# Gates with tokens on the partitions in two blocks, values ahead of keys, embedding pieces in pairs of one bank

## What is computed

```python
for i in range(2):
    h = rms_norm(x, g_pre_mix[i])
    if i == 0: mix = short_conv_mixer(h, ...)
    else:
        k, v = split(rms_norm(x, g_kv) @ w_kv)           # 1024 key and 1024 value columns
        mix = diff_attention(h, k, v, dist_bias, w_q, lambda, ...)   # 8 heads, keys of 2 x 64
    x = x + rms_norm(mix, g_post_mix[i])
    x = x + rms_norm(conv_ffn(rms_norm(x, g_pre_ffn[i]), ...), g_post_ffn[i])
    gate = sigmoid(rms_norm(x, g_pre_ple[i]) @ w_gate)   # 1024 x 1024
    x = x + rms_norm(gate * (p_i @ w_proj), g_post_ple[i])   # p_i: 256 features, w_proj 256 x 1024
```

## Time and profile before

| | us |
|---|---|
| median of 3 runs | 1263.34 (1263.01 to 1263.54) |
| the profiled execution, span | 1261.9 |
| TensorE busy | 1231.6 |
| VectorE busy | 908.1 |
| ScalarE busy | 737.1 |

### The profile page before, as it was taken

The page is one execution under the profiler, slowest core; times in us unless marked ns, Lnnn a source line. Parts: engine busy times, 40 slices in busy tenths (PEclk is TensorE's granted clock), DMA queues, the critical chain, the costliest instruction groups (busy, mean ns, idle before and its releaser), DMA issues.

```text
span 1261.9 us, 24318 instructions
## 1 busy us (share of the span) xinstructions
PE 1231.6 (98%) x10110; PEld 1206.4 (96%) x10110; DVE 908.1 (72%) x1571; ACT 737.1 (58%) x1257; POOL 6.4 (1%) x16
## 2 busy tenths in 40 slices
PE   8999999999999999999999999999999999999997
PEld 8889799999999999999999999999888899999997
DVE  6896566665446776444876899966788768999656
ACT  6753456664445765334555666655766866665655
POOL 1000000000000000000000000000000000000000
PEclk9999999999999999999999999999899999999999
DMA  7223244555552655553663666574364236665640
GB/s 275 72 101 105 64 164 148 192 181 180 174 168 98 216 186 185 184 184 126 218 195 119 193 194 199 159 238 134 120 225 159 89 117 192 193 189 188 215 141 34
DMA packets 59753, 205.51 MB, mean 163 GB/s; under 512 B 6739, under 2 KB 9340, under 8 KB 59516
## 3 DMA queue, kind: packets, MB, share of 16 engines
q1 hardware_dynamic: 57536, 201.21, 49.0%
q10 hardware_dynamic: 2108, 2.75, 0.7%
HBM read 202.87 MB, written 1.06 MB: 162 GB/s over the span
## 4 chain that ended last, share of the span: by engine, by line
PE 85%; DVE 8%; ACT 4%; issue 1%; DMA 1%; DVEq 0%; ACTq 0%
PE PS L368 69%; PE PS L413 6%; DVE WL L353 2%; PE PS L380 2%; DMA RAW<-wpack 1%; ACT WH L346 1%; PE PS L462 1%; PE PS L2450 1%; ACT EE L2608 1%; PE PS L520 1%; PE PS L2517 0%; PE PS L688 0%; DVE X L1905 0%; ACT L532 0%; PE PS L402 0%
## 5 line engine op out<-in xcount | busy, mean ns | idle before, releaser
L353 DVE TENSOR_TENSOR WL<-RAW,WH 128x1024 fp32r<-128x1024 f32 (+2 forms) x387 | 460.6, 1195 | 211.3 <-ACT WH L346 210.8
L346 ACT ACTIVATE WH<-RAW 128x1024 fp32r<-128x1024 f32 (+2 forms) x387 | 392.3, 1033 | 218.6 <-PE PS L368 184.8
L368 PE MATMUL PS<-UH,WH 128*128 128x256 f32 (+1 forms) x1464 | 415.7, 284 | 7.6 <-DVE WL L353 3.8
L368 PE MATMUL PS<-UL,WH 128*128 128x256 f32 (+1 forms) x1464 | 414.9, 283 | 0.0
L368 PE MATMUL PS<-UH,WL 128*128 128x256 f32 (+1 forms) x1464 | 414.7, 283 | 0.0
L368 PEld LDWEIGHTS PS<-UH,WH 128*128 128x128 f32 x1464 | 276.6, 189 | 8.6 <-issue 3.4
L368 PEld LDWEIGHTS PS<-UH,WL 128*128 128x128 f32 x1464 | 276.9, 189 | 0.0
L368 PEld LDWEIGHTS PS<-UL,WH 128*128 128x128 f32 x1464 | 275.2, 188 | 0.0
L368 PE MATMUL PS<-HL,WH 128*128 128x272 f32 (+1 forms) x512 | 145.8, 285 | 0.0
L368 PE MATMUL PS<-HH,WH 128*128 128x272 f32 (+1 forms) x512 | 145.6, 284 | 0.0
L368 PE MATMUL PS<-HH,WL 128*128 128x272 f32 (+1 forms) x512 | 145.4, 284 | 0.0
(11 more groups left out here) (409 smaller groups left out, 2066.1 us busy)
## 6 DMA issues: line engine op xcount, KB each, us to landing
RAW<-wpack SPq DMA_DIRECT2D x361, 512.0 KB, 4.2
RAW<-wpack SPq DMA_DIRECT2D x18, 384.0 KB, 3.5
RAW<-wpack SPq DMA_DIRECT2D x6, 256.0 KB, 2.7
C<-cst SPq DMA_DIRECT2D x1, 1072.0 KB, 5.9
HB<-bias_rows ACTq DMA_DIRECT2D x1, 1024.0 KB, 5.3
out<-X SPq DMA_DIRECT2D x4, 256.0 KB, 2.3
X<-xin ACTq DMA_DIRECT2D x2, 272.0 KB, 6.0
X<-xin SPq DMA_DIRECT2D x2, 272.0 KB, 5.9
```

The lines of the kernel that those rows point to most:

```text
L346: a.e.activation(WH[n % NH][:, 0:w], RAW[n % NR][:, 0:w], ACT.Copy).then_inc(*a.mark("wh", n))
L353: v.e.tensor_tensor(WL[n % NH][:, 0:w], RAW[n % NR][:, 0:w], WH[n % NH][:, 0:w].bitcast(f32), ALU.subtract).then_inc(*v.mark("wl", n))
L368: ins = t.e.matmul(o, part(n, hw, kw, a, b), x(kx), start=first and not i and not p, stop=last and i == len(kcs) - 1 and p == 2)
```

## The change

**Embedding.** Two pieces share a bank, with tokens on the partitions: for each block i of 128 tokens 256 columns of w_proj move. Six pieces are now done ahead of the FFN and two ahead of the gate, and ScalarE copies a pair in one instruction. The turn of the banks is set again at a later unit of the FFN.

**Gate.** A unit is now two 128-row pieces of w_gate by 512 columns. The tokens of a block are stationary and 512 weight columns move. First both blocks for the columns 0 to 511 (h = 0), then block 0 and then block 1 for the columns 512 to 1023 (h = 1). The norm's factor is a scale of the sigmoid, per partition, so that the spread and the multiplication L2349 go; the sum of squares over the features is an accumulator of one ScalarE and one VectorE instruction per block. Each block is then scaled and turned by eight transposes (`gate_turned`) into features on partitions and added to X (`gate_added`). In layer 0, block 0 is turned inside the last products of block 1; block 1 is turned inside the first value products.

**Values ahead of keys.** Behind the gate of layer 0 come four value units (heads 0 to 3, block 0 and then block 1), then four key units; the keys of heads 4 to 7 take the place of the first four half value units in the loop over the heads, in bank 1 or 2.

```diff
+            pairs_of_rows("v", "w_kv_2", None, 1024, 1536)
+            proj("k", "w_kv_2", None, 0, 512)
+            for h in range(8):
+                proj("q", "w_q_2", 0, 128 * h, 128 * h + 128)
+                if h < 4:
+                    proj("k", "w_kv_2", None, 512 + 128 * h, 640 + 128 * h)
...
 # tensor_ffn
-            embed(2, 5)
+            embed(2, 6)
...
-                        if (u, m) == (3, 0):
+                        if (u, m) == (4, 0):
                             banks.go_on((banks.at["root", prev] + 1) % 8)
...
-            keep_going(t, 2, f"f{layer}")
+            keep_going(t, 8, f"f{layer}")
...
+            for k in range(8):
+                gate_rows(0, k, (0, 1))
+            for k in range(8):
+                if k == 2:
+                    root_sum(t, st, 0, S, ("rs", st))
+                gate_rows(1, k, (0,))
+            if layer:
+                for k in range(8):
+                    gate_rows(1, k, (1,), 0, 256)
+            for k in range(8):
+                if k == 6 - 2 * layer:
+                    gate_turned(t, layer, 0)
+                gate_rows(1, k, (1,), 256 * layer, 512)
 # scalar_ffn
-            act_split(a, n0 + NH)
+            act_split(a, n0 + NH + 4)
             root_sqrt(a, st, S)
             preload(a, ACT.Sigmoid)
...
+            gate_sigmoid(a, layer, 0, 0, 0, 512)
+            gate_sigmoid(a, layer, 1, 0, 0, 512)
             gate_square(0)
             gate_square(1)
+            gate_sigmoid(a, layer, 0, 1, 0, 512)
+            preload(a, ACT.Sqrt, 61)
+            gate_root(a, layer, 0)
+            gate_scale_first(a, layer, 0)
+            preload(a, ACT.Sigmoid, 62)
 # vector_ffn
+            dve_split(v, n0 + NH + 4)
             root_recip(v, st, S)
-            dve_split(v, n0 + NH)
+            gate_product(v, layer, 0, 0, 0, 512)
+            gate_product(v, layer, 1, 0, 0, 512)
+            gate_first_sum(v, layer, 0)
+            gate_first_sum(v, layer, 1)
+            gate_product(v, layer, 0, 1, 0, 512)
+            gate_squares(v, layer, 0)
+            gate_recip(v, layer, 0)
+            gate_scale_second(v, layer, 0)
 # tensor_diff, after the two blocks of values (gate_turned(t, 0, 1) ahead of k = 6 of block 0)
+            pair, spare = banks.at["nt", 0, 1], banks.at["nt", 0, 0]
+            for j in range(4):
+                b = banks.put(t, (spare, spare + 1, *rest)[j], ("k", j), ("kh", j))
...
+                if j == 1:
+                    banks.go_on(pair)
+                    root_sum(t, "kv", 0, S, ("rk", "kv"))
             b = banks.take(t, ("lam",), ("lame",))
 # scalar_diff (high(i, j) waits for X of block i, piece j, and makes UH; 128 columns)
+            act_split(a, n0)
+            for j in range(3):
+                high(0, j)
+            gate_sigmoid(a, 0, 1, 1, 0, 512)
+            preload(a, ACT.Sqrt, 63)
+            high(0, 3)
+            gate_root(a, 0, 1)
+            high(0, 4)
+            gate_scale_first(a, 0, 1)
...
             for j in range(8):
                 split_hi(a, ("qx", j), XH[:, j, :], X_(j), g("gpm1", j))
+                if j == 1:
+                    root_sqrt(a, "kv", S)
+                if j in (2, 4, 6):
+                    act_split(a, n0 + 2 + j // 2)
             a.e.dma_start(HB[:, :, :], rows).then_inc(*a.mark_dma("hb"))
             root_keep(a, "kv", 0, S)
+            for i in range(2):
+                a.e.activation(V[:, i, 0:512], PS[:, banks.at["v", 0, i], :], ACT.Copy, scale=rooted("kv", 1 + i))
+            act_split(a, n0 + 4 + NH)
             scalar_embed(a, 1)
             a.wait_ge("dif", "lam")
             a.e.activation(SM[:, 38:40], PS[:, banks.at["lam",], 0:2], ACT.Exp)
 # vector_diff
+            for j in range(4):
                 key(j)
+                dve_split(v, n0 + NH + 1 + j)
             vector_embed(v, 1)
 # tensor_end, scalar_end, vector_end
+            keep_going(t, 20)
+            for j in range(8):
+                ins = t.e.matmul(..., MR[:, 1, 128 * j:128 * j + 128], DG, start=True, stop=True)
```

More of the change, by code:

```diff
@@ L2089, in embed @@
                 for j in range(j0, j1):
[L2090 to L2096, removed]
+                    i, x, at = j % 2, (0, 0, 1, 2)[j // 2], (0, 256, 0, 0)[j // 2]
+                    n = unit_at["ple", 3 * layer + x]
+                    b = banks.at["ple", layer, j - 1] if i else banks.take(t, ("ple", layer, j), ("pe", layer, j + 1))
+                    t.wait_ge("wl", n)
+                    t.wait_ge("ul", "p", layer)
+                    for k in range(2):
+                        for p, (y, hw) in enumerate(((PH, 1), (PL, 1), (PH, 0))):
+                            ins = t.e.matmul(PS[:, b, 256 * i:256 * i + 256], y[:, k, 128 * i:128 * i + 128], part(n, hw, k, at, at + 256),
+                                             start=k == 0 and p == 0, stop=k == 1 and p == 2)
+                    if i:
+                        ins.then_inc(*t.mark("ple", layer, j))
+                    if j in (3, 5, 7):
                         sig.also(("used", n), ("ple", layer, j))
@@ L2141, in tensor_ffn @@
             root_end(t, f"f{layer}", 1, S)
-            embed(5, 6)
+            embed(6, 7)
             root_spread(t, f"f{layer}", S)
-            embed(6, 8)
-            keep_going(t, 2, f"f{layer}")
+            embed(7, 8)
+            keep_going(t, 8, f"f{layer}")
             n0 = unit_at["gate", 8 * layer]
[L2147 to L2163, removed]
-                            *t.mark("gate", layer, u, m))
-                for m in range(2):
-                    sig.also(("used", n + m), ("gate", layer, u, m))
@@ L2440, in value @@
             def value(s):
+                if s < 4:
+                    key(4 + s, banks.put(t, BV + s % 2, ("k", 4 + s), ("kh", 4 + s)))
+                    return
                 uu, half = s // 2, s % 2
@@ L2566, in scalar_diff @@
             a.e.dma_start(HB[:, :, :], rows).then_inc(*a.mark_dma("hb"))
-            root_sqrt(a, "kv", S)
-            act_split(a, n0 + NH + 1)
             root_keep(a, "kv", 0, S)
-            act_split(a, n0 + NH + 4)
+            a.wait_ge("rr", "kv")
+            for i in range(2):
+                a.wait_ge("dif", "v", 0, i)
+                a.e.activation(V[:, i, 0:512], PS[:, banks.at["v", 0, i], :], ACT.Copy, scale=rooted("kv", 1 + i)).then_inc(
+                    *a.mark("v", 0, i))
+            act_split(a, n0 + 4 + NH)
             scalar_embed(a, 1)
```

353 lines of the change are left out of this document (202 added, 151 removed).

## The result

| | us |
|---|---|
| before, median of 5 runs on the same chip | 1263.34 (1262.01 to 1263.54) |
| after, median of 5 runs | 1267.79 (1267.06 to 1269.39) |
| ratio | 1.0042, interval 1.0029 to 1.0054 |
| span of the profiled execution after | 1265.3 |

The changed kernel is 4.45 us slower. The forecast was 1272, in a range from 1263 to 1276; the sign was right, the size twice too large.

What follows compares the result with a forecast made beforehand. It took TensorE's matmuls (1416 in 167.29 us) to bound the kernel; +0.8 + 11.8 - 1.5 + 1.5 - 3.6 = +9.0 on the 1263.3 median gave 1272.3, say 1272 us, in a range from 1263 to 1276.

Steps and rivals of the forecast that it cites:

- Step 1: Embedding: six pieces instead of five ahead of each FFN, +0.4 us a layer, +0.8 in all (bounds 0 and 1.4).
- Step 2: Gate of layer 0: two late-loaded units hold the root until 893.5; TensorE stands still 6.2 us inside the gate.
- Step 3: Values behind layer 0's gate: start 906.4, waits of 1.9 and 1.0 us between block 0's pieces, end 921.4.
- Step 4: Keys behind the values: K2's high part stands behind the root, a wait of 1.7 us; keys and `lam` end 936.6.
- Step 5: First query: waits for `lam`'s exponential behind six splits, starts at 946.7 (bounds 944.5 and 948) against 934.92, +11.8 us.
- The clock term: Behind the hole ahead of query 0: about 4 us of work at half pace, +1.5 us (0 to 2).
- The covered waits: Behind query 0: the idle 0.47 us at 941.20 and 1.01 at 951.90 go, -1.5 us.
- Step 6: Last gate and tail: no wait for block 0, last addition 1255.5 against 1259.1, -3.6 us (bounds -2.5 and -4.5).
- the forecast proper: Whole kernel: the forecast's own band of 1266.5 to 1276 us, given a chance of 0.64.
- the signs that it had named: TensorE idle about 6 us ahead of the transposes and 10 ahead of query 0; root behind two copies waiting for DMA.
- The table loads: New ScalarE table switches: the skill's draining would add some 4 us, making 1276; left out, 1.28 us a load taken.

Runs made afterwards that it cites:

- Experiment 2: Changed kernel with the gate root behind four unit splits instead of six, units 9 and 10 split later: 1266.47 us, ratio 1.0028.
- experiment 4: Kernel before with the new form in layer 1 alone (embedding pairs, gate by blocks, new tail), layer 0 old: 1259.04 us, ratio 0.9966.
- experiments 1 to 3: Changed kernel with `lam` in bank 5 (1260.97 us), with the gate root ahead of two later unit splits (1266.47), and with both edits (1258.69).
- experiment 1: Changed kernel with the product `lam` put in bank 5 instead of bank 0: 1260.97 us, ratio 0.9987.
- experiments 2, 6, 7 and 8: The sixth: on version 3, K2's split ahead of the `kv` root (1257.40 us), then VectorE's keys before splits (1256.14), then query 1 and head 0 earlier (1258.08).
- version 3: Changed kernel with both edits, `lam` in bank 5 and the gate root ahead of the splits of units 9 and 10: 1258.69 us, ratio 0.9968.
- the best version: version 3 with K2's split ahead of the `kv` root and VectorE's key and query 0 copies ahead of later low parts: 1256.14 us, ratio 0.9951.
- experiment 7: the best version with the third and fourth value unit splits moved between the pieces of the additions: 1260.03 us, ratio 0.9982.
- experiment 8: Kernel before with `lam` in bank 0: 1268.52 us; the same with the bank turn kept: 1262.74; changed kernel with `lam`'s exponential ahead of five splits: 1261.48.

## Why the prediction was right or wrong

The forecast's times count from a gate of layer 0 that starts at 873.69. In the trace after it starts at 872.52, so 1.2 us of each difference between two such times is not the forecast's.

**Step 1, embedding: too high.** +0.8 forecast. The FFN of layer 0 starts 0.5 us later measured from the short convolution's output, that of layer 1 0.25 later, and each gate then starts 0.3 earlier: about +0.2. The fillers that took the place of two pieces ahead of the gate gave a little back; I had put them at 0.

**Step 2, gate of layer 0: right in kind, a little high.** Two copies wait for DMA ahead of the root, as written. The second copy ended and the root began at 891.79 where I had 893.5; from the gate's start this is 19.3 us against 19.8. The wait ahead of the transposes is 5.26 (forecast 6.2). Unit 9 was loaded from 885.25 and copied from 888.43, 3.2 us, where I had taken 4.5. But unit 10 decided when the root came: it was issued at 886.39 and copied from 890.83, 4.4 us later, the lower end of what I had allowed it. Experiment 2, which brought the transposes 3.1 us forward, shows what that was worth: 1.8 us of time (1.1 of distance), not 3.5 to 5, since the rest went into what stood behind it.

**Step 3, values: right.** Start 904.48 (906.4), waits of 1.40 and 0.49 (1.9 and 1.0), end 919.1 (921.4). My VectorE addition of 128 columns from PSUM, taken as 0.27, has that pace in the tail: eight in 2.16 us.

**Step 4, K2: right.** A wait of 1.43 against 1.7, for the reason given.

**Step 5, first query: the right place and reason, 30% too large.** The bank count by hand was right: `lam` in the query's bank. The wait is 8.36 us (10), query 0 at 942.71 (946.7); from the gate's start the loss is 8.96 us (11.8). Of the missing 2.8 us half came before the load: N+10 was issued at 935.01, which is 62.5 us behind the gate's start where I had 63.9, since the root, the values and K2 were each a little earlier. The other 1.2 are the load: it was copied at 939.60, 4.6 us after its issue, where I had taken 5.8 from a load that had stood behind others. The clock term (+1.5) measured 2.0: 20 products from 942.71 to 947.14 took 0.213 us each where 0.117 is the pace. The covered waits (-1.5) were right, and the two terms of opposite sign made the stretch behind the query even, to within half a microsecond.

**Step 6, tail: right, a little low.** -3.6 forecast, -4.5 in the traces, -4.3 by experiment 4. The products ended as before; the chain behind them took 6.6 us where I had 6.9, and the span ended 2.4 us behind the last addition instead of 2.8 as before.

**Sum.** +0.2 + 9.0 + 0 - 4.5 = +4.7 against a measured +4.45; forecast +9.0. The missing 4.3 are 2.8 at query 0, 0.9 in the tail and 0.6 at the embedding. The three errors have the same sign, so nothing cancelled; the term that was sized worst is that of query 0. The bounds of step 5 (944.5 to 948) were too narrow: both ends assumed a late load, and from the gate's start query 0 came 0.6 us below the lower one. The result lies 1.3 us above the lower end of the forecast proper (1266.5), and the range given (1263 to 1276) held because it was wide. What speaks for the working are the signs that it had named, the two waits with their releasers and the two copies ahead of the root, and not the time.

**The table loads.** In the changed kernel a table load runs from 892.05 to 893.33 and the next instruction starts at 893.35. The Trainium skill, "ScalarE: Activation LUTs", section "What ACT_TABLE_LOAD costs", adds some 1.38 us of draining to each switch. The trace again does not agree, and the 1276 that this would have given did not come.

**What I had not asked.** Whether the loss could be had back. I treated the late exponential and the late root as what the change is; experiments 1 to 3 show that they are two places in an order, worth 9.3 us, and that the form itself is neutral in layer 0 (within 0.3 us in the traces) and worth 4.3 us in the tail.

## What to carry to other kernels

Where an engine runs in written order, a wait needs two things: a late event and something that is queued or banked behind it. Look for what else shares the bank or the queue of a small side product, and move that, before the big work is moved. A rotating allocator couples far places: an edit that takes one slot less moved a 4.9 us wait into a stage 80 us later, so compare the whole timeline, not the edited stretch. And a removed wait is worth what the next wait leaves of it. In experiment 2 a wait of 5.26 us shrank to 2.17, which gave 1.1 to 1.8, because a fixed wait stood behind. A wait of 8.36 us, with 2 us of lower clock behind it, gave 6.9 in experiment 1, the rest going into two new waits of 1.40 and 1.96. Read the granted clock behind each wait that you make or move: in experiments 2, 6, 7 and 8 the lower level stood behind such a wait and took 1 to 3 us.

## What the runs showed of the hardware

A hole in TensorE's work can cost more than its length: behind 8.36 idle us 20 products ran at a granted clock of 0.50, 2 us extra, and with matmuls in the hole at 1.00. Behind equal short holes the clock did not do the same each time: after 2.15 idle us the eight transposes took 1.06 us in version 3 and 1.73 us in the best version, whose order up to there is the same. In experiment 7 the clock was at 0.50 from 907.7 to 914.0, behind a wait of 2.21. Of two loads of 512 KB issued 1.1 us apart (885.25 and 886.39) the first was used 3.2 us later and the second 4.4. A table load can be hidden in a wait: in experiment 8 it ran at 932.37, while ScalarE would have waited for `lam` until 934.1 anyway.
